# Expert units beside the gates' build: three products of 224 columns instead of one of 448 and one of 224

## What is computed

```
def block(args):
    xb, ib, gb = args
    hid = jnp.einsum('thkd,td->thk', u[ib], xb)
    a = jax.nn.gelu(hid.astype(jnp.float32), approximate=False) * gb
    return jnp.einsum('thk,thkd->td', a.astype(x.dtype), v[ib])
```

## Time and profile before

| what | us |
|---|---|
| median of 3 runs | 1648.49 |
| lowest and highest run | 1645.3, 1649.43 |
| span of the profiled execution | 1646.3 |

### The profile page before, as it was taken

One profiled execution on the slowest core, in us unless ns is written; L12 is line 12 of the kernel. 1 busy time (PEld: TensorE's weight loads), 2 busy tenths in 40 slices (PEclk: granted clock), 3 DMA queues, 4 the chain that ended last, 5 costly groups with the idle time before them and its releaser, 6 DMA issues.

```text
span 1646.3 us, 30255 instructions
## 1 busy us (share of the span) xinstructions
PE 1621.1 (98%) x10334; PEld 1482.8 (90%) x10334; DVE 1034.2 (63%) x2292; ACT 978.3 (59%) x1972; POOL 1133.3 (69%) x897
## 2 busy tenths in 40 slices
PE   8999999999999999999999999999999999999999
PEld 8888888889998888799998999999999999999998
DVE  2794432334343333746443398988999988889997
ACT  5646655555465555665643777676555566666664
POOL 8455799998989999887654699999899811112210
PEclk9999999999999999999999999999999999999999
DMA  7333455555555555454352467666778788899995
GB/s 234 105 111 108 154 190 185 187 191 167 186 172 186 186 190 191 156 186 133 120 201 77 140 212 217 202 200 221 239 251 255 249 298 285 272 306 316 331 339 175
DMA packets 104318, 334.38 MB, mean 203 GB/s; under 512 B 12144, under 2 KB 26608, under 8 KB 103952
## 3 DMA queue, kind: packets, MB, share of 16 engines
q1 hardware_dynamic: 94368, 294.99, 53.6%
q0 software_dynamic: 9696, 37.91, 7.8%
q10 hardware_dynamic: 144, 0.08, 0.0%
HBM read 324.90 MB, written 7.47 MB: 202 GB/s over the span
## 4 chain that ended last, share of the span: by engine, by line
PE 86%; POOL 6%; DVE 3%; issue 3%; ACT 2%; DMA 0%; POOLq 0%; SPq 0%; DVEq 0%; ACTq 0%
PE bank L786 21%; PE bank L818 19%; PE bank L1447 10%; PE bank L819 9%; PE banks_and L786 6%; POOL w_lo L694 6%; PE bank L1449 5%; PE banks_and L1447 3%; PE bank L1424 2%; PE banks_and L1449 2%; PE bank L764 1%; PE banks_and L1336 1%; PE banks_and L1424 1%; PE banks_and L865 1%; ACT w_hi L1502 1%
## 5 line engine op out<-in xcount | busy, mean ns | idle before, releaser
L694 POOL TENSOR_TENSOR w_lo<-ring,w_hi 128x512 fp32r<-128x512 f32 x804 | 1041.2, 1313 | 231.4 <-ACT w_hi L1502 196.3
L1502 ACT ACTIVATE w_hi<-ring 128x512 fp32r<-128x512 f32 x1060 | 663.3, 630 | 516.9 <-PE bank L819 240.8
L818 PE MATMUL bank<-h_high_and_low,w_hi 128*128 128x448 f32 (+1 forms) x1728 | 582.2, 388 | 1.3 <-POOL w_lo L694 1.3
L819 PE MATMUL bank<-h_high_and_low,w_lo 128*128 128x224 f32 (+1 forms) x1728 | 466.8, 270 | 0.0
L818 PEld LDWEIGHTS bank<-h_high_and_low,w_hi 128*128 128x128 f32 x1728 | 324.3, 188 | 51.2 <-POOL w_lo L694 4.7
L819 PEld LDWEIGHTS bank<-h_high_and_low,w_lo 128*128 128x128 f32 x1728 | 328.0, 190 | 1.6
L786 PE MATMUL bank<-h_high_and_low,w_hi 128*128 128x256 f32 x1296 | 245.7, 287 | 4.5 <-DVE arena L2280 2.2
L1447 PE MATMUL bank<-A_high_and_low,w_hi 128*128 128x448 f32 x768 | 248.6, 375 | 0.0
L786 PEld LDWEIGHTS bank<-h_high_and_low,w_hi 128*128 128x128 f32 x1296 | 206.6, 193 | 7.3 <-issue 2.6
L1449 PE MATMUL bank<-A_high_and_low,w_lo 128*128 128x224 f32 x768 | 202.0, 263 | 0.0
L2845 DVE TENSOR_TENSOR w_lo<-ring,w_hi 128x512 fp32r<-128x512 f32 x256 | 176.2, 689 | 27.3 <-ACT w_hi L1502 16.4
(11 more groups left out here) (455 smaller groups left out, 2371.4 us busy)
## 6 DMA issues: line engine op xcount, KB each, us to landing
ring<-stream SPq DMA_DIRECT2D x530, 512.0 KB, 3.5
spill<-mask_parts SPq DMA_DIRECT2D x56, 112.0 KB, 3.0
XN<-spill SPq DMA_DIRECT2D x56, 112.0 KB, 5.9
arena<-branch_w POOLq DMA_DIRECT2D x1, 3072.0 KB, 13.1
X<-x SPq DMA_DIRECT2D x2, 512.0 KB, 4.6
arena<-kv_w SPq DMA_DIRECT2D x1, 1024.0 KB, 8.0
out<-X SPq DMA_DIRECT2D x4, 256.0 KB, 2.1
arena<-row POOLq DMA_DIRECT2D x1, 512.0 KB, 4.8
```

Source lines behind the costliest of these rows:

```text
L694: nc.gpsimd.tensor_tensor(w_lo[:, hs, :], ring[:, slot(phase, e), k * HALF:(k + 1) * HALF], w_hi[:, hs, :].bitcast(F32), ALU.subtract) \
L818: mm(dst[:, 0:2 * n], high, h[:, k, :, 0:n], start=k == 0, stop=False, skip_group_check=True)
L819: last = mm(dst[:, 0:n], low, h_hi[:, k, 0:n], start=False, stop=k == KC - 1, skip_group_check=True)
L1502: A(w_hi[:, half_slot(phase, e, k), :], ring[:, slot(phase, e), k * HALF:(k + 1) * HALF], ACT.Copy).then_inc(rounded, 1)
```

## The change

The units of `peer_build` use a new function `feature_tokens`, which issues `passes` on 224 columns for each chunk: three matmuls with three weight loads, all into columns 0 to 223. The bank then holds the finished sum. ACT's copy of the other half (L1996) and DVE's addition (`summed_build`, L2817) are gone. The gelu of unit n-1 waits for PE's end of that unit, where it waited for DVE's addition, and the wait for the free slot in `stage` moved to it. The first 72 units and the units of `v` stay as they are.

```
+            def feature_tokens(dst, phase, e, i, n):
+
+                for half in range(2):
+                    pe.wait_ge(*half_split(phase, e, i, half))
+                    for c in range(4):
+                        k = 4 * half + c
+                        last = passes(dst[:, 0:n], weights(phase, e, half, slice(c * P, (c + 1) * P)),
+                                      (h_hi[:, k, 0:n], h_lo[:, k, 0:n]), k == 0, k == KC - 1)
+                    last.then_inc(halves_used, 1)
...
-                        feature_apart(bank(f"build{c % 3}"), "peer_build", g, i, n=T)
+                        feature_tokens(bank(f"build{c % 3}"), "peer_build", g, i, T)
...
-                    act.wait_ge(ev("build_sum"), c + 1)
+                    act.wait_ge(*unit_used("peer_build", c % BUILD_UNITS, c // BUILD_UNITS))
+                    if c >= STAGED:
+                        act.wait_ge(ev(f"spilled{c % STAGED}"), 16 * (c // STAGED))
...
-                    if n >= STAGED:
-                        act.wait_ge(ev(f"spilled{n % STAGED}"), 16 * (n // STAGED))
-                    act.wait_ge(*unit_used("peer_build", g, i))
-                    A(stage[:, n % STAGED, :], bank(f"build{n % 3}")[:, T:2 * T], ACT.Copy).then_inc(ev("build_low"), 1)
...
-                def summed_build(n):
-
-                    i, g = n // BUILD_GROUPS, n % BUILD_GROUPS
-                    dve.wait_ge(*unit_used("peer_build", g, i))
-                    dve.wait_ge(ev("build_low"), n + 1)
-                    hidden = bank(f"build{n % 3}")[:, 0:T]
-                    V.tensor_tensor(hidden, hidden, stage[:, n % STAGED, :], ALU.add).then_inc(ev("build_sum"), 1)
...
-                    summed_build(n - 2)
...
-                summed_build(GROUPS_OF_4 - 2)
...
-                summed_build(GROUPS_OF_4 - 1)
```

## The result

| | before | after |
|---|---|---|
| median, us | 1647.25 (4 runs) | 1657.79 (4 runs) |
| lowest and highest run | 1645.3, 1649.43 | 1654.73, 1659.91 |
| span of the profiled execution | 1646.3 | 1652.6 |

The ratio is 1.0064, with a 95% interval of 1.0051 to 1.0077. The changed kernel is slower by 0.64%, which is more than the 0.3% that a measurement can tell. The forecast was 1657.7 us, or +0.56%.

What follows compares the result with a forecast made beforehand. PE was taken as the bound: +9.7 us for the units' added loads and -0.45 us at the hand-over make +9.25 us, a span of 1655.6 and a median of 1657.7 us (+0.56%), range 1650.5 to 1665.

Steps and rivals of the forecast that it cites:

- PE sets the pace of the stage: In the 56 groups PE waits for nobody; a group takes 3.40 us, 0.90 scatter and 2.50 unit.
- 24 x 0.1117 = 2.680 us for a unit: PE, the unit: 24 loads at a floor of 0.1117 us, up from 2.507 us; +9.7 us for 56 units.
- The bounds of 0.100 and 0.120: Lowest and highest price in us of one unit matmul on PE: -6.0 us or +20.5 us in all.
- The scatter at nothing: PE, the scatter: the same four matmuls, eight records, 0.893 us, so no cost from the change.
- DVE's and ACT's removed steps at nothing: In the groups, 21.6 us of DVE additions and 19.0 us of ACT copies go, off the path, gaining nothing.
- The hand-over at -0.45 us: At the start of the units of `v`, the removed copy and addition lay on the path: 0.45 us saved.
- From the span to the median: The median, 1648.49 us, lies 2.2 above the profiled span; keeping that turns a span of 1655.6 into 1657.7 us.
- The rival of a fixed cost: PE's unit: fixed cost per matmul, no load floor, 0.1067 us each; stage +3.0 us, result 1651.0 us, chance 0.14.
- The rival of DVE: In the groups: DVE is the bound after all, so the change helps with shorter groups; chance next to nothing.

Runs made afterwards that it cites:

- pair_no_sum: Kernel before with only ACT's copy and DVE's addition removed, matmuls of 448 and 224 columns kept: 1646.95 us, ratio 0.9994.
- three_widths: Kernel after with the unit's matmul columns going round eight widths from 64 to 256; one run for distances, not time: 0.1117 us between loads up to 224.
- three_with_sum: Kernel after with the third matmul into columns of its own and ACT's copy and DVE's addition back: 1657.71 us, 1.0057 of the kernel before.
- pair_bf16_scatter: Kernel before (448 and 224 columns, copy and addition kept) with the scatter's one-hots and gates in bf16: 1668.81 us, ratio 1.0127.
- three_bf16_scatter: Kernel after with the scatter's one-hots and gates in bf16: 1661.59 us, 1.0081 of the kernel before.
- three_bf16_shared: Kernel after with bf16 scatter, DVE instead of POOL making the second half's low part in every second unit: 1648.58 us, 1.0002 of the kernel before.
- the fastest kernel: Kernel after with bf16 scatter, DVE making the second half's low part for two units of five, ahead of the one-hots: 1636.02 us, 0.9930 of before.

## Why the prediction was right

- **PE sets the pace of the stage.** Right. PE waits for nobody in the kernel after either, and taking two engines' work away alone (pair_no_sum) left 3.400 us.
- **24 x 0.1117 = 2.680 us for a unit.** Right, and for the reason given, a row of loads on their floor: the chain shows 2.68, a group is 3.573 us, and the stage is longer by 200.10 - 190.40 = 9.7 us, as forecast. The bounds of 0.100 and 0.120 were each refuted at 224 columns: no width from 64 to 224 goes under 0.1117 (three_widths), and 0.120 is found at 256 alone.
- **The scatter at nothing.** Right, 0.90 us.
- **DVE's and ACT's removed steps at nothing.** Right, by three_with_sum, which has them and the same 3.573 us a group.
- **The hand-over at -0.45 us.** Right in the trace, with the low activations in time (they end at 1325.59, and PE's second unit starts at 1326.07). No median could show it; three_with_sum has the copy and the addition at the hand-over again, and pair_no_sum is without them and without the jump.
- **From the span to the median.** The sum was added to a median of 1648.49. That 1657.79 then lies 0.1 us from the 1657.7 of the forecast is luck: the four runs spread over 5.2 us, and the median of before was 1647.25 with a fourth run. The difference of the medians is 10.5 us where 9.25 was forecast, and the traces give 9.05 for the stage and what follows it. The profiled execution after is 3.1 us faster than its median, and 2.8 us ahead of the one before when the early units begin, so the check of the steps had to be made on the stages and not on the spans. By the spans alone (+6.3) one would have found (6.3 + 0.45) / 56 + 2.507 = 2.628 us for a unit, and 0.1095 for a load.
- **The rival of a fixed cost.** It would have given 3.45 us a group. The step by which it fails is its extrapolation: the width below 256 columns doesn't lower the cost by 0.4167 ns a column, but by 0.008 us in all, down to the floor.
- **The rival of DVE.** Next to nothing was right for this kernel. But where PE does wait for DVE, in the kernels with a bf16 scatter and a short product, the kernel with the change is 6 us faster.

What the prediction did not see: DVE's product and POOL's low parts got longer, though DVE has less to do. The groups of the stage after, and POOL's low parts by duration (least, median and most in ns):

```profile
L694 POOL TENSOR_TENSOR w_lo<-ring,w_hi 128x512 fp32r<-128x512 f32 x111 | 161.1, 1465 | 11.4 <-ACT w_hi L1512 10.2
...
L2786 DVE SCALAR_TENSOR_TENSOR arena<-arena 128x1024 f32<-128x1024 f32 x20 | 44.2, 2212 | 0.0
```

```profile
L694 POOL TENSOR_TENSOR w_lo<-ring,w_hi x111: 1273/1291/2264, 1123.0 to 1317.3; 128x512 fp32r<-128x512 f32 x111
```

Before, the means were 1325 and 1902 ns. The trace shows how, in each of the 20 groups with a product alike:

```profile
1144.52 3.51 POOL L694 TENSOR_TENSOR w_lo<-ring,w_hi 128x512 fp32r<-128x512 f32 x2 [0.76 <-ACT w_hi L1512]
...
1144.66 2.21 DVE L2786 SCALAR_TENSOR_TENSOR arena<-arena 128x1024 f32<-128x1024 f32 x1
```

The product begins 0.14 us behind a low part of 1.28 us and ends 1.08 after that one's end. The low part behind it has its record from 1145.80 on, and it takes 2.23. So each product is held up by about 1 us and then holds up the next low part by about 1 us. Here the product came in between two low parts, where in pair_bf16_scatter it had to wait for several; what decides that, no run shows. In pair_no_sum, with DVE's additions gone as well, the products take 2.86 us on average. It costs nothing in either, since PE is the bound.

## What to carry to other kernels

Count loads and not only columns: in these rows a matmul cost about the greater of its load and its stream, so a split that keeps the columns is dear as soon as the parts are shorter than a load. To see whether work removed from another engine is worth anything, look at whether the engine on the chain ever waits for it; if not, even 40 us of it are worth nothing. And before making the bound engine faster, look at what the next ones do to each other when they are full: an engine that is at 90% may have its gaps just where another needs them.

## What the runs showed of the hardware

- **A load of 128 columns of 32-bit weights takes 0.1117 us in a row of loads**, with 2, 64, 128, 192, 208, 216 and 224 moving columns, for new weights and for the same again, and into any of the columns tried. At 240 columns a matmul takes 0.1122 us, at 256 it takes 0.120. The kernel's transposes (L764), which move 128 columns, stand 0.109 apart.
- **With bf16 weights the distance from one scatter matmul to the next is about 0.06 us**, half of that floor; the row of four with 0.38 to 0.40 us shows it, of which the last matmul's own 0.22 is the end: 0.16 to 0.18 us for three distances. The Trainium skill ("TensorE: Matmul & The Clock Gate", section "Weight-path perf modes — Fast Weight Load (FWL) and DoubleRow") says that loads of 128 columns are quicker for types other than FP32. These rows agree with it.
- **DVE's product with both inputs in SBUF can be put off for as long as POOL's subtractions follow each other without a gap**: 1.21 us alone, 6.45 and up to 10.3 us beside them, and with 64 columns 0.20 alone and up to 9.3. In the kernel after it waited for one subtraction only, 2.21 us in all. DVE's own subtraction (the low part) took 0.69 us at the hand-over and 1.20 on average in the stage, beside POOL.
- **A stop of PE is paid twice.** TensorE's granted clock is 1.00 (2.4 GHz) up to the stop of 3.67 us in pair_bf16_scatter. Behind it three pairs still take 0.32 to 0.39 us each, and then the clock is at the lower level, 1.2 GHz, for some 3 us. The windows of the stop and of what follows (columns as in the earlier trace rows), and two long matmuls there:

```profile
1149.00:1153.00 4.00, 0.34 (x6) 0.22 (x5) 4.00 (x9) 1.39 (x3) 3.26 (x3) 1.00 0.50 144
1153.00:1157.00 4.00, 4.00 (x20) 3.55 (x18) 4.00 (x10) 1.24 (x3) 1.41 (x2) 0.62 0.37 121
```

```profile
1154.06 0.61 PE L818 MATMUL bank<-h_high_and_low,w_hi 128*128 128x448 f32 x1
...
1156.41 0.60 PE L818 MATMUL bank<-h_high_and_low,w_hi 128*128 128x448 f32 x1
```

Four pairs take 2.35 us, 0.588 each where a pair takes 0.313: 1.1 us lost on these four alone. Over the stage (1124 to 1330 us) the mean clock was 0.91 in this kernel and 0.92 in three_bf16_scatter; in the kernels with the short product it was 0.98, and in three_bf16_shared and in the fastest kernel 1.00. So part of the loss of the first two is the clock's, as a consequence of the stops; 18.5 and 16.5 us are the estimates above, and no run took the two parts apart.
